# Reordering the filler projections under the two attentions of a float32 two-block transformer kernel

## The reference, cut to what matters

```python
a_q, a_k, a_v, a_f, b_q, b_k, b_v = split_cols(h @ w_in, EVEN_SIZES)
aq, ak = rms_norm(a_q...), rms_norm(a_k...)
a_out = forgetting_attention(aq, ak, av, cum_logf)        # 8 heads of 64
bq, bk = rms_norm(b_q...), rms_norm(b_k...)
bq, bk = apply_partial_rope(bq, cos, sin), apply_partial_rope(bk, cos, sin)
b_out = differential_attention(bq, bk, bv, lam)           # 4 heads, two softmaxes each
b_out = rms_norm(b_out, subln_gain) * (1.0 - lambda_init)
return jnp.concatenate([a_out, b_out], axis=-1) @ w_out
```

```python
k, v = split_cols(mem_n @ w_kv, (D_MODEL, D_MODEL))
```

## Time and profile before

| | |
|---|---|
| runs of the kernel before | 2342.36, 2347.71, 2350.39 us (median 2347.71) |
| the profiled execution's own time | 2358.14 us |
| its span, first to last instruction | 2356.3 us |
| mean granted TensorE clock | 0.98 of full speed |
| busy: PE, DVE, ACT, POOL | 2251.9, 1530.4, 1176.3, 125.3 us |
| weights moved | 389.34 MB read, 166 GB/s over the span |

### The profile page before, as it was taken

How to read it: one execution, slowest core, us unless ns; L and a number is a source line. 1 busy time by engine, 2 the same in 40 slices (tenths; PEclk the granted TensorE clock), 3 DMA queues, 4 the chain that set the end, 5 groups by cost and what they waited for, 6 DMA issues and landing times.

```text
span 2356.3 us, 44939 instructions
## 1 busy us (share of the span) xinstructions
PE 2251.9 (96%) x18378; PEld 2185.4 (93%) x18378; DVE 1530.4 (65%) x2331; ACT 1176.3 (50%) x1792; POOL 125.3 (5%) x146
## 2 busy tenths in 40 slices
PE   6999998999999999999999999998999999898998
PEld 6999887899999999799999999987999999898998
DVE  6766567676667655676666666667666666656664
ACT  5644444564456445345554554435544544526443
POOL 2000000110011001010000000000000000001001
PEclk9999998999999999999999999999999999999999
DMA  7556432365555557343665665633565665533653
GB/s 239 182 180 186 142 108 72 99 202 183 179 185 175 192 184 219 108 153 101 195 197 180 196 197 184 206 108 110 177 191 176 189 196 188 161 126 122 196 186 106
DMA packets 383626, 393.28 MB, mean 167 GB/s; under 512 B 6768, under 2 KB 381680, under 8 KB 383296
## 3 DMA queue, kind: packets, MB, share of 16 engines
q1 hardware_dynamic: 381504, 383.30, 50.8%
q0 software_dynamic: 1920, 7.11, 1.0%
HBM read 389.34 MB, written 1.05 MB: 166 GB/s over the span
## 4 chain that ended last, share of the span: by engine, by line
PE 85%; DVE 7%; ACT 5%; issue 2%; POOL 1%; DMA 1%; SPq 0%; POOLq 0%; ACTq 0%; DVEq 0%
PE acc L570 25%; PE acc L574 24%; PE acc L571 24%; DVE w_lo L1235 2%; ACT w_hi L923 2%; PE acc L588 2%; PE acc L589 2%; PE acc L590 2%; DVE hn_lo L1277 1%; POOL t L1704 1%; PE wide L697 1%; DMA raw<-in_ffn_w_in 1%; PE wide L721 1%; PE wide L752 0%; PE wide L656 0%
## 5 line engine op out<-in xcount | busy, mean ns | idle before, releaser
L1235 DVE TENSOR_TENSOR w_lo<-raw,w_hi 128x1024 fp32r<-128x1024 f32 (+2 forms) x774 | 895.5, 1160 | 537.0 <-ACT w_hi L923 534.3
L923 ACT ACTIVATE w_hi<-raw 128x1024 fp32r<-128x1024 f32 (+2 forms) x774 | 777.2, 1008 | 929.6 <-PE acc L574 830.0
L570 PE MATMUL acc<-hn_hi,w_hi 128*128 128x256 f32 x3536 | 857.6, 283 | 48.0 <-DVE hn_lo L1277 23.4
L571 PE MATMUL acc<-hn_lo,w_hi 128*128 128x256 f32 x3536 | 845.8, 280 | 0.0
L570 PEld LDWEIGHTS acc<-hn_hi,w_hi 128*128 128x128 f32 x3536 | 672.3, 190 | 59.3 <-issue 17.6
L571 PEld LDWEIGHTS acc<-hn_lo,w_hi 128*128 128x128 f32 x3536 | 672.8, 190 | 1.1 <-issue 0.5
L574 PE MATMUL acc<-hn_hi,w_lo 128*128 128x256 f32 x3536 | 483.8, 280 | 0.0
L574 PEld LDWEIGHTS acc<-hn_hi,w_lo 128*128 128x128 f32 x3536 | 444.1, 190 | 0.0
L570 PE MATMUL acc<-hid_hi,w_hi 128*128 128x256 f32 x1408 | 334.5, 278 | 0.0
L571 PE MATMUL acc<-hid_lo,w_hi 128*128 128x256 f32 x1408 | 334.5, 278 | 0.0
L571 PEld LDWEIGHTS acc<-hid_lo,w_hi 128*128 128x128 f32 x1408 | 265.4, 188 | 0.0
(11 more groups left out here) (239 smaller groups left out, 1979.3 us busy)
## 6 DMA issues: line engine op xcount, KB each, us to landing
raw<-in_ffn_w_in SPq DMA_DIRECT2D x88, 1024.0 KB, 5.1
raw<-in_ffn_w_out SPq DMA_DIRECT2D x32, 1024.0 KB, 5.3
raw<-in_ffn_pre_w_gate SPq DMA_DIRECT2D x22, 1024.0 KB, 5.3
raw<-in_ffn_pre_w_up SPq DMA_DIRECT2D x22, 1024.0 KB, 5.4
raw<-in_ffn_post_w_gate SPq DMA_DIRECT2D x22, 1024.0 KB, 5.3
raw<-in_ffn_post_w_up SPq DMA_DIRECT2D x22, 1024.0 KB, 5.4
raw<-in_x_w_kv SPq DMA_DIRECT2D x16, 1024.0 KB, 5.5
raw<-in_ffn_pre_w_down SPq DMA_DIRECT2D x16, 1024.0 KB, 5.2
```

The source lines that it names most:

```text
L570: nc.tensor.matmul(bank, wh[:, j, :], a_hi[:, u.k0 + j, :], start=u.first and j == 0, stop=False)
L571: nc.tensor.matmul(bank, wh[:, j, :], a_lo[:, u.k0 + j, :], start=False, stop=False)
L923: nc.scalar.activation(w_hi[:, u.slot, 0:u.nk, :], raw[:, u.raw % RING, 0:u.nk, P * u.half:P * u.half + P], ACT.Copy).then_inc(w_hi_ready, 1)
L1235: nc.vector.tensor_tensor(w_lo[:, u.slot, 0:u.nk, :], raw[:, u.raw % RING, 0:u.nk, P * u.half:P * u.half + P], w_hi[:, u.slot, 0:u.nk, :]. ...
```

## The change

Two parts of one reordering. In the stream, the projections bq, bk and bv of the second attention come ahead of the memory keys. In the order, the first head norm and the first attention take bq, bk and bv as fillers; the second head norm and the rotation take the memory keys; the second attention takes all memory values and the first half of the output product.

```diff
             add("af", [(w, 1536)], KB, "F", "hn", gen, width=P)
-            project(w, ("aq", 0, 512), ("ak", 512, 512), ("av", 1024, 512))
+            project(w, ("aq", 0, 512), ("ak", 512, 512), ("av", 1024, 512),
+                    ("bq", 1544, 512), ("bk", 2056, 512), ("bv", 2568, 512))
             add("memk0", cols(kv, 0, D), KB, "F", "mn", fill)
-            project(w, ("bq", 1544, 512), ("bk", 2056, 512), ("bv", 2568, 512))
...
-                    head(work[:, 16:24, :], 8, 64, ["even"] * 4 + [("even", 1)] * 4, memk[0:2], memk[2:5])
-                    att("A", spread(memk[5:8] + span("bq", "bk")))
-                    bv, memv, half = span("bv"), span("memv0"), span("mixout0a")
-                    head(work[:, 24:32, :], 8, 64, [("even", 2)] * 4 + [("even", 3)] * 4, bv[0:2], bv[2:4] + memv[0:2])
-                    rotate(work[:, 24:32, :], perm_rope, rope_c, rope_s, memv[2:4])
-                    att("B", [memv[4:6], memv[6:8], [(0, 4)], half[0:1], half[1:2], half[2:3], half[3:4], [], [], [], []])
+                    bq, bk, bv = span("bq"), span("bk"), span("bv")
+                    memv, half = span("memv0"), span("mixout0a")
+                    head(work[:, 16:24, :], 8, 64, ["even"] * 4 + [("even", 1)] * 4, bq[0:2], bq[2:4] + bk[0:1])
+                    att("A", spread(bk[1:4] + bv))
+                    head(work[:, 24:32, :], 8, 64, [("even", 2)] * 4 + [("even", 3)] * 4, memk[0:2], memk[2:5])
+                    rotate(work[:, 24:32, :], perm_rope, rope_c, rope_s, memk[5:8])
+                    att("B", [memv[0:2], [], memv[2:4], [], memv[4:6], [], memv[6:8] + [(0, 4)], half[0:1], half[1:3], half[3:4], []])
                     head(cat[:, 4:8, :], 4, 128, ["subln"] * 4, half[4:6], half[6:8])
                     split_cat(4, 8)
```

## The result

| | before | after |
|---|---|---|
| median of the runs (7 each) | 2350.39 us | 2364.48 us |
| range of the runs | 2342.36 to 2362.36 | 2356.43 to 2367.56 |
| ratio | | 1.0066, 95% interval 1.0033 to 1.0098 |
| profiled execution, span | 2358.14, 2356.3 us | 2358.85, 2357.0 us |

The change makes the kernel slower: the medians differ by 14.1 us, the ratio stands for 15.5; 10.7 were forecast. In the changed kernel every line behind 423 is one higher, and in some experiments a few more.

What follows compares the result with a forecast made beforehand. TensorE, busy for 96% of the span, was taken as the bound. First attention −3.4, second +12.4, clock −7.5 and +9.2 summed to +10.7 us on a median of 2347.7: 2358.4 us (+0.45%), range 2348 to 2367.

Steps and rivals of the forecast that it cites:

- Waits in A: First attention with 7 units in 11 steps: TensorE's waits sum to 10.6 us where 2.3 were, +8.3.
- step 3: First attention, behind empty step 2 with VectorE late from the head norm: TensorE waits 3.7 us.
- step 6: First attention, behind one unit and an empty step: chain 4.95 us less 3.0 covered, a wait of 2.0.
- step 8: First attention, behind bv0, bv1 and empty step 7: chain 6.05 us less 2.15 covered, a wait of 3.9.
- Waits in B: Second attention with four units more: TensorE's waits sum to 9.0 us where 8.3 were, +0.7.
- The hole isn't filled: Second attention: its 8.3 us of idle time stays despite more units, since VectorE and ScalarE make it before each PV.
- clock term of B: Second attention: only its 3.8 us wait lowers the clock, costing 3.1 us; the old falls' 7.5 us go.
- the waits of 2.3: Second attention, step 6, behind memv4 and memv5: a 2.3 us wait, clock cost taken as 0, at most 3.4.
- those of 1.1 and 1.8: Second attention, steps 7 and 8: waits of 1.1 and 1.8 us behind the concat split, no clock cost counted.
- the 7.5 us: Second attention: the kernel before's two waits cost 3.4 + 4.1 us at the lower clock, which go: −7.5.
- The first: Rival, whole kernel: faster, empty steps cost only TensorE's own work, clock holds; −10.6 us, 2337 us, chance 0.09.
- The second: Rival, whole kernel: no change, waits as forecast but clock stays up or falls once briefly; 2347 to 2352 us, chance 0.24.

Runs made afterwards that it cites:

- e5: Changed kernel's first attention kept, its four units moved to second head norm and rotation, second attention as before; stretch 150.1 us, ratio 1.0114 to before.
- e3: Changed kernel with 20, 24, 24 and 14 idle matmuls in the four long waits of its two attentions; stretch 143.0 us, ratio 1.002 to before.
- e6: Kernel before with 14, 13 and 15 idle matmuls in its three waits over 3 us; stretch 131.2 us, ratio 0.998.
- e1: Kernel before with only bq and bk ahead of the memory keys in the stream, steps equally full; stretch 136.5 us, ratio 0.9991.
- e7: Kernel before with two units instead of four moved from first to second attention, first's last two steps empty; stretch 133.7 us, ratio 1.0014.
- e2: Changed kernel with the first attention's seven units bunched in steps 6 to 10, steps 0 to 5 empty; stretch 145.1 us, ratio 1.0048 to before.
- e4: Changed kernel with evacuations and splits moved behind the next step's bias, exponential and copy in both attentions; stretch 144.9 us, ratio 1.0029 to before.
- e9: Kernel before with the late splits of e4 in both attentions; stretch 136.4 us, ratio 1.0021.
- e10: Kernel before with the idle matmuls of e6 and the late splits of e4 in the first, odd mixer's and third attentions; stretch 128.6 us, ratio 0.9932.

## Why the prediction was right, and where its terms were off

**The direction and the mechanism** held. The forecast was 10.7 us and the stretch shows 15.7; the measured ratio is 1.0066 where 1.0046 was forecast, and its interval holds both. That the sum isn't further off is partly luck, as shown below.

**Waits in A:** forecast 10.6, traced 11.2 (step 3: 3.7 and 3.28; step 6: 2.0 and 2.09; step 8: 3.9 and 4.08; step 2: 1.0, but 0.86 and 0.88, since the scores of item 2 waited as well). With the clock this gave "near 54 us" for A; it took 54.1. e5 measured the price of thinning A by itself, 13.3 us; my terms were 8.3 + 6.2.

**Waits in B:** forecast 9.0, traced 9.4 (3.8 and 4.16; 2.3 and 2.44; 1.1 and 1.21; 1.8 and 0.80; two small ones of 0.34 and 0.44 that I hadn't seen). "The hole isn't filled" was right.

**The term that was mis-sized is the clock term of B.** I had said "B near 50 us"; it took 57.9. The size of one fall was right: the windows of the five falls give 2.9 to 3.5 us each, and I had taken 3.1. Their number was wrong. A has the two that I had counted (6.2 forecast, 6.1 by e3). B has three, and I had let only the wait of 3.8 us cost anything; the waits of 2.3 stood "at 0, bounded above by 3.4 each", and those of 1.1 and 1.8 weren't counted for the clock at all. Both groups have a fall (windows 388.70 and 402.40), so the clock cost B 8.4 us by e3 instead of 3.1. And the 7.5 us that the kernel before got back are 6.4 by e6; some 2 of them lie behind B, in the tail, which is 1.9 us shorter, so they couldn't shorten B itself.

Put together, the difference of the clock terms is 14.5 − 6.4 = 8.1 us where the sum had 1.7, and the waits have 10.0 (20.6 − 10.6) where it had 9.0. These two make 18.1; the stretch has 15.7. The other 2.4 us are TensorE's own work. Without idle matmuls and at full clock it is busy for 113.0 us in e3's stretch and for 115.4 in e6's, with 816 matmul rows in both, where I had let four units less in A and four more in B cancel out. Why the same matmuls took less time stays open. It hid part of the miss of 6.4 us in the clock term.

The page that I had weighed, the Trainium skill (TensorE: Matmul & The Clock Gate, section "HAM oscillation — how this bites in real kernels"), has the clock fall behind gaps in the matmuls. This case's runs agree: with the gaps filled (e3, e6) the granted clock stays at 1.00, and the changed kernel's stretch is 9.0 us shorter.

**The rivals.** The first needed waits under 1 us in A's empty steps; three were 2 to 4 us. The second needed a clock that stays up; it was 0.84 and 0.82. That the stream's order has a price of its own is excluded by e1 for bq and bk; the place of bv wasn't tried alone.

## What to carry to other kernels

Where a filler unit brings work for the other engines along, count the chain from its end through their queues: taking a filler out of a step saves its 2.9 us only if TensorE has other work to cover that chain. Here A lost four units worth 11.7 us and became 2.6 us longer: the time came back first as waits and then again at the lower clock. Filling every step with a bias behind it (before, e7) beats spreading few units, and so does bunching them (e2), by 4.4 us here. The order within a queue can be worth as much as the placement of the fillers: bias before splits took 7.1 us off the changed kernel, and 2.6 off A in the kernel before, but it loses where a split that TensorE needs at once comes a step later (waits of 4.5 and 4.7 us, e4 and e9). A wait of a few us that can't be filled with work can be filled with idle matmuls that end before it does: in the kernel before this took 5.1 us off the stretch (e6).

## What was not expected of the hardware

**The same matmuls run at two rates while the granted clock reads 1.00.** The first feed-forward layer is the same code in both kernels. The groups of TensorE's instructions from 100 to 150 us, kernel before:

```profile
L570 PE MATMUL acc<-hn_hi,w_hi 128*128 128x256 f32 x141 | 34.1, 281 | 0.0
```

Changed kernel, same stretch:

```profile
L571 PE MATMUL acc<-hn_hi,w_hi 128*128 128x256 f32 x147 | 34.3, 276 | 0.0
```

In 50 us one execution issues 426 matmul rows and the other 444, so 4% more; e2 (443) and e10 (444) ran like the second, e3 and e6 (427 each) like the first. It changes from stage to stage within an execution, with no wait and no lower clock in the profile: from 1900 to 1960 us it is the other way round, 532 rows of 276 ns before and 512 of 281 ns in the changed kernel. At the start of A the changed kernel is 5.5 us ahead (272.14 and 277.68), and over the whole span the stages outside the stretch make up for its 15.7 us (2356.3 and 2357.0). Whether it also makes the scatter of the whole times, from 2342 to 2362 us in seven runs of the kernel before, isn't shown. What sets the rate wasn't tried.

**The clock fell behind short waits as well.** In e4 A has six waits, none over 1.6 us, yet its mean clock was 0.83; the changed kernel's last fall in B came behind a wait of 1.21. In the kernel before, A with 1.3 and 1.0 stayed at 1.00, and the changed kernel's wait of 2.09 had no fall behind it. So the length of the last wait alone doesn't tell whether the clock falls; what does was not isolated.
